# Rounded head outputs in the latents' tiles, a written bank order, and moved transposes and masked copies in layers 2 and 3 of a four-layer model on one core

## The chip, the cores and the metric

The kernel runs on one core of a Trainium2 chip. The metric is the device time of one execution in microseconds: everything from the inputs in device memory to the output in device memory, measured over several runs. The profile is that of one further execution.

## What is computed

A token sequence of 256 positions and width 1024 goes through four layers in fp32. Layers 0 and 1 are one kind of block (adaptive modulation, windowed attention with sinks, a pooling mixer, a gated feed-forward). Layers 2 and 3 are the other kind, and the change is in them alone:

```python
for l in range(DEPTH):
    h = rmsnorm(x, attn_norm[l])
    z = h @ w_in[l]
    (c_q, c_kv, k_rope, g_q, g_k, g_v, g_lr, g_g, r_q, r_k, r_v, r_g) = jnp.split(z, split_points, axis=-1)
    y_a = mla_branch(c_q, c_kv, k_rope, ...)      # 4 heads: queries, keys and values from normalized latents
    y_a = head_rmsnorm(y_a, mla_out_norm[l]).reshape(B, S, MLA_HEADS * MLA_V)
    y_b = gla_branch(g_q, g_k, g_v, g_lr, g_g, ...)   # gated linear attention, 4 heads
    y_c = retention_branch(r_q, r_k, r_v, r_g, ...)   # retention with fixed decay, 4 heads
    x = x + jnp.concatenate([y_a, y_b, y_c], axis=-1) @ w_out[l]
    h = rmsnorm(x, ffn_norm[l])
    u = h @ ffn_w_up[l]
    a, bv = u[..., :D_FF_2], u[..., D_FF_2:]
    a = causal_dwconv(a, ffn_conv_w[l], ffn_conv_b[l])
    x = x + (jax.nn.silu(a) * bv) @ ffn_w_down[l]
```

The first branch is softmax attention over latents (256 positions, two blocks of 128 queries); each of the other two ends in a normalization over its heads and a multiplication with silu of a gate.

## The kernel before, in words

**Products.** Every large fp32 product is made of three matmuls on operands that are split in a high part, rounded to the reduced fp32 form, and a low part, the rest: high by low, low by high, high by high (`exact`, L490 to L492). Weights stream through four raw slots. For each unit of weights ScalarE writes the high half (`prepare`, L1133) and VectorE the low half (`lo`, L1576), two instructions of 1024 columns each; TensorE waits for the second low half (`weights`). A raw slot is loaded again by SyncE once VectorE's low halves are done. Activations are split in the same way, into `in_hi` and `in_lo`, or for the latents into `cn_hi` and `cn_lo`. Small products (scores, rotations, transposes) are plain fp32: `group` (L497), `transposes` (L539), the two rotations (L828, L833).

**The order of the work** is written out by hand, for each engine apart; engines meet by semaphores. In `attention_mixed`, TensorE's order in each of layers 2 and 3 is: latents turned, `gqk`, `rqk`, the rope part of the queries (`qr`) and the rest (`qn`), keys `kn` and values `vm` out of one unit `ukv`, three blocks of attention scores, the gate logits (`ggate`), the values `gv`, the retention scores (four, from the masked keys `kbd`, which lie in `c_row`), the values `rv`, the head outputs of retention (`rout`, L879 and L880), the gate scores (four, from `kbd` again), the attention outputs (from `probT2`), the head outputs of the gate branch (`gout`), the gate product 0 (`gg`), four sums of squares over the heads (L928), the gate product 1 (`rg`), and the output projection `into_y` with the units `wo` 0, 1, 3, 2. Between these stand the transposes of the three blocks of probabilities, `turn_prob(0)` to `turn_prob(2)`.

**Banks.** `take` gives each product the next bank of a rotation that `banks(...)` sets, and waits until the former tenant of the bank has been read. The rotation in this stretch is 4, 5, 1, 0, 3, 2, 6, 7, over and over.

**VectorE** rotates the retention queries and keys, writes the four masked copies `kbd` (L1958), then the low halves of `ukv`; it scales scores and finds their extremes (`softmax`, L1732, L1735), divides by the sums (`normalize`, L1739, L1741; its result is what `turn_prob` waits for), makes the gate queries and keys (L1993, L1999), and at the end scales the head outputs (`head_norm`, L2016) and writes their low parts (`cat_lo`, L1722). **ScalarE** makes the exponentials, copies banks to memory (L1211), takes the root of the sums of squares (L1456, L1459) and rounds the scaled head outputs into `in_hi` (`round_cat`, L1216). The head outputs are eight tiles: 0 to 3 of the attention, 4 and 5 of the gate branch, 6 and 7 of retention. `in_hi` and `in_lo` hold the layer's normalized input until the last gate product has read it, so ScalarE waits for that product before it rounds the first tile:

```python
                sc.wait_ge(*due("gate", L, 1))
                round_cat(L, (0, 1, 2, 3))
```

`cn_hi` and `cn_lo` are five tiles each, whose place in memory the probabilities `prob2` and their transposes `probT2` use after the latents; the last reader of those are the attention outputs.

## Time and profile before

| | |
|---|---|
| median of 3 runs | 1191.18 us (1190.67 to 1191.89) |
| the profiled execution | 1190.44 us, span 1188.6 us from first to last instruction |
| TensorE busy | 1145.2 us, 96% of the span |
| VectorE busy | 809.1 us, 68% |
| ScalarE busy | 634.3 us, 53% |
| GpSimd busy | 25.6 us, 2% |
| mean granted clock of TensorE | 0.998 |
| layer 2, attention part | about 590 to 690 us |
| layer 3, attention part | about 895 to 995 us |

The profiler's names: PE is TensorE, DVE VectorE, ACT ScalarE, SP SyncE, POOL GpSimd. Times count from the span's start. A row of the view in order of time gives start, duration, engine, line, operation, output and inputs, shapes, a count of merged instructions and, in brackets, the idle time before it and what ended that. Matmuls overlap: a row's duration is longer than the distance to the next start, and their ends are modelled. An fp32 matmul shows as two.

### The profile page before, as it was taken

The page shows a single profiled execution, that of the slowest core. Times are in us where ns is not written, and L with a number is a line of the kernel's source. Part 1 is how long each engine was busy: PE and PEld are TensorE (multiplying, and loading weights), DVE is VectorE, ACT ScalarE, POOL GpSimd, SP SyncE. Part 2 cuts the span into 40 slices and gives each one's busy share as a digit, 9 for nine tenths or more (in the row PEclk, how much of TensorE's full clock was granted, in tenths as well). Part 3 has the DMA queues.
Part 4 walks back from the last instruction along what each step waited for, and adds up shares of the span by engine and source line. Part 5 has one row for each costly group of instructions (what it writes and reads, how often), then busy time and mean ns, then how long its engine had stood idle before and what let it go on. Part 6 is the DMA issues. An engine that isn't in the chain of part 4 may idle for free.

```text
span 1188.6 us, 19635 instructions
## 1 busy us (share of the span) xinstructions
PE 1145.2 (96%) x7899; PEld 1024.6 (86%) x7899; DVE 809.1 (68%) x1255; ACT 634.3 (53%) x1114; POOL 25.6 (2%) x61
## 2 busy tenths in 40 slices
PE   5989999999999999999999999999999999999997
PEld 3556999998878999999888799999989889999996
DVE  5798966797986755655676667666566757765663
ACT  3067443456557644435655766555556577555543
POOL 2200000000000000000000000000000000000000
PEclk9999999999999999999999999999999999999999
DMA  9994999997543766585343355544544434555530
GB/s 376 410 420 193 333 324 298 320 377 277 190 154 117 282 236 227 206 265 174 126 178 107 142 206 183 207 178 178 180 141 156 144 106 178 212 179 190 198 106 36
DMA packets 37305, 252.97 MB, mean 213 GB/s; under 512 B 4416, under 2 KB 4704, under 8 KB 8928
## 3 DMA queue, kind: packets, MB, share of 16 engines
q1 hardware_dynamic: 34992, 244.47, 57.2%
q0 software_dynamic: 2080, 7.25, 1.6%
q8 instruction: 63, 1.03, 0.4%
q14 instruction: 26, 0.21, 0.1%
q10 hardware_dynamic: 144, 0.00, 0.0%
HBM read 250.64 MB, written 1.06 MB: 212 GB/s over the span
## 4 chain that ended last, share of the span: by engine, by line
PE 84%; DVE 8%; DMA 3%; ACT 3%; issue 1%; SPq 0%; DVEq 0%; ACTq 0%
PE bank L490 25%; PE bank L492 25%; PE bank L491 25%; PE bank L497 3%; DMA raw_w<-weights 3%; DVE raw_w L1586 2%; PE bank L585 2%; PE bank L539 2%; DVE lo_w L1576 2%; PE bank L628 1%; ACT gtok L1138 1%; PE bank L928 1%; DVE prob L1732 1%; DVE tok L1795 0%; DVE smax L1735 0%
## 5 line engine op out<-in xcount | busy, mean ns | idle before, releaser
L1576 DVE TENSOR_TENSOR lo_w<-raw_w,hi_w 128x1024 fp32r<-128x1024 f32 (+3 forms) x346 | 408.9, 1209 | 124.3 <-ACT hi_w L1133 123.8
L1133 ACT ACTIVATE hi_w<-raw_w 128x1024 fp32r<-128x1024 f32 (+3 forms) x346 | 350.5, 1041 | 151.3 <-DMA raw_w<-weights 88.2
L490 PE MATMUL bank<-in_hi,lo_w 128*128 128x256 f32 x1408 | 395.8, 281 | 0.0
L491 PE MATMUL bank<-in_lo,hi_w 128*128 128x256 f32 x1408 | 392.9, 279 | 0.0
L492 PE MATMUL bank<-in_hi,hi_w 128*128 128x256 f32 x1408 | 392.9, 279 | 0.0
L490 PEld LDWEIGHTS bank<-in_hi,lo_w 128*128 128x128 f32 x1408 | 264.3, 188 | 2.5 <-issue 0.8
L491 PEld LDWEIGHTS bank<-in_lo,hi_w 128*128 128x128 f32 x1408 | 263.6, 187 | 1.9 <-issue 0.5
L492 PEld LDWEIGHTS bank<-in_hi,hi_w 128*128 128x128 f32 x1408 | 264.7, 188 | 0.0
L490 PE MATMUL bank<-hi_w,in_lo 128*128 128x256 f32 (+2 forms) x464 | 143.9, 310 | 8.6 <-DVE in_lo L1687 2.4
L492 PE MATMUL bank<-hi_w,in_hi 128*128 128x256 f32 (+2 forms) x464 | 141.0, 304 | 0.0
L491 PE MATMUL bank<-lo_w,in_hi 128*128 128x256 f32 (+2 forms) x464 | 140.8, 303 | 0.0
L490 PE MATMUL bank<-hi_w,hid_lo 128*128 128x512 f32 x352 | 139.5, 396 | 0.5 <-DVE hid_lo L2059 0.5
L491 PE MATMUL bank<-lo_w,hid_hi 128*128 128x512 f32 x352 | 139.0, 395 | 0.0
L492 PE MATMUL bank<-hi_w,hid_hi 128*128 128x512 f32 x352 | 139.0, 395 | 0.0
L1586 DVE SCALAR_TENSOR_TENSOR raw_w<-raw_w,c_row 128x1024 f32<-128x1024 f32 x96 | 113.5, 1221 | 25.1 <-DMA raw_w<-weights 24.7
L490 PEld LDWEIGHTS bank<-hi_w,in_lo 128*128 128x128 f32 x464 | 87.8, 189 | 17.8 <-issue 9.0
L492 PEld LDWEIGHTS bank<-hi_w,in_hi 128*128 128x128 f32 x464 | 87.9, 189 | 4.6
L491 PEld LDWEIGHTS bank<-lo_w,in_hi 128*128 128x128 f32 x464 | 87.9, 189 | 4.2
L492 PEld LDWEIGHTS bank<-hi_w,hid_hi 128*128 128x128 f32 x352 | 66.1, 188 | 16.0
L490 PEld LDWEIGHTS bank<-hi_w,hid_lo 128*128 128x128 f32 x352 | 66.1, 188 | 15.2 <-DVE hid_lo L2059 0.6
L491 PEld LDWEIGHTS bank<-lo_w,hid_hi 128*128 128x128 f32 x352 | 66.1, 188 | 14.2
L1494 ACT ACTIVATE shared<-bank,vcol 128x256 f32<-128x256 f32 x44 | 24.8, 564 | 98.6 <-PE bank L492 90.8
(216 smaller groups left out, 1080.0 us busy)
## 6 DMA issues: line engine op xcount, KB each, us to landing
raw_w<-weights SPq DMA_DIRECT2D x215, 1024.0 KB, 5.7
ink<-ink_w SPq DMA_DIRECT2D x8, 640.0 KB, 13.2
rows<-norm_rows POOLq DMA_DIRECT2D x5, 512.0 KB, 4.9
ink<-whole_w SPq DMA_DIRECT2D x2, 1024.0 KB, 23.1
early_out<-whole_w SPq DMA_DIRECT2D x2, 1024.0 KB, 13.9
rows<-mod_rows POOLq DMA_DIRECT2D x4, 512.0 KB, 9.2
raw_w<-weights SPq DMA_DIRECT2D x2, 832.0 KB, 4.4
const<-const_table SPq DMA_DIRECT2D x1, 1538.0 KB, 8.0
```

Source lines behind the costliest of these rows:

```text
L490: nc.tensor.matmul(o, st[1], mv[0], start=start, stop=False, **kw)
L491: nc.tensor.matmul(o, st[0], mv[1], start=False, stop=False, **kw)
L492: return nc.tensor.matmul(o, st[0], mv[0], start=False, stop=stop, **kw)
L497: last = nc.tensor.matmul(o, w, r, start=(i == 0), stop=(i == len(pairs) - 1))
L539: last = nc.tensor.transpose(b[:, P * i:P * (i + 1)], s_, k("ident"))
L585: done = nc.tensor.matmul(ps(job)[:, :], half(raw[:, 2 * u + n, :], T), whole[u][:, n, cols(c)], start=(u == 2 and n == 0), stop=(u == 1 a ...
L628: last = nc.tensor.matmul(b[:, P * i:P * (i + 1)], modcol[:, ROWS[(L, kind, w)], t:t + 1].to_broadcast([P, P]), k("ident"), start=True, st ...
L928: nc.tensor.matmul(b[:, :], k(ones), head_sq[:, m, :], start=True, stop=True).then_inc(*sig("hsum", L, n))
L1133: nc.scalar.activation(hi_w[:, m % NSPLIT, cut], raw_view(unit)[:, cut], ACT.Identity).then_inc(*sig("hi_w", unit, i))
L1494: nc.scalar.activation(conv[:, f % 2, :], ps(("gu", L, f))[:, 0:256], ACT.Identity, bias=v(f"conv_b{l}", f), scale=v(f"conv_w{l}", 44 + f) ...
L1576: nc.vector.tensor_tensor(lo_w[:, m % NSPLIT, cut], raw_view(unit)[:, cut], hi_w[:, m % NSPLIT, cut].bitcast(F32), ALU.subtract).then_inc( ...
L1586: ins = nc.vector.scalar_tensor_tensor(w, w, 1.0, c_row[:, :], ALU.mult, ALU.mult, accum_out=mods[:, l, 2 * n + f:2 * n + f + 1])
```

## The change

Five things, all in `attention_mixed` of layers 2 and 3.

1. The rounded head outputs of tiles 0 to 3 and their low parts go to `cn_hi` and `cn_lo`; the units `wo` 0 and 1 of the output projection read them there. ScalarE's wait for the last gate product in front of the rounding is gone. Tiles 4 to 7 go to `in_hi` and `in_lo` as before.
2. The rotation of banks is a list of 31 numbers, one for each product from `rqk` to `gout`.
3. TensorE's order: `turn_prob(1)` stands right behind the `rv` product, ahead of the wait for the copy of its result; `turn_prob(2)` stands ahead of the gate scores.
4. With it, ScalarE copies the second transposes ahead of the high halves of `wo` 0, and VectorE normalizes block 2 ahead of the gate queries and keys.
5. VectorE writes the low halves of `ukv` ahead of the masked keys of retention.

```diff
-            def mixed_wait(L):
-                return (lambda t: pe.wait_ge(*due("cat_lo", L, t))), (lambda t: t), both
+            def mixed_wait(L, unit):
+
+                return (lambda t: pe.wait_ge(*due("cat_lo", L, t))), (lambda t: t), ((cn_hi, cn_lo) if L >= 2 and unit[2] < 2 else both)
...
-                banks(4, 5, 1, 0, 3, 2, 6, 7)
+                banks(4, 5, 1, 0, 3, 2, 6, 7, 4, 5, 1, 0, 3, 2, 6, 7, 4, 5, 1, 0, 2, 3, 6, 0, 7, 4, 5, 1, 2, 3, 0)
                 product(("rqk", L), ("rqk", L, 0), both)
...
                 turn_prob(0)
                 token_values("rv")
+                turn_prob(1)
                 pe.wait_ge(*due("rv_in", L))
                 head_outputs(("rout", L), "ratt", 256)
-                turn_prob(1)
+                turn_prob(2)
...
                     last.then_inc(*sig(*job))
-                turn_prob(2)
...
-            def round_cat(L, tiles):
+            def round_cat(L, tiles, dst):
                 for t in tiles:
                     sc.wait_ge(*due("cat_raw", L, t))
-                    nc.scalar.activation(in_hi[:, t, :], raw[:, t, :], ACT.Identity).then_inc(*sig("cat_hi", L, t))
+                    nc.scalar.activation(dst[:, t, :], raw[:, t, :], ACT.Identity).then_inc(*sig("cat_hi", L, t))
...
                 values("rv", 256)
+                probT_in(1)
                 prepare(("wo", L, 0))
                 head_in(("rout", L), 3)
-                probT_in(1)
                 probT_in(2)
...
-                sc.wait_ge(*due("gate", L, 1))
-                round_cat(L, (0, 1, 2, 3))
+                round_cat(L, (0, 1, 2, 3), cn_hi)
...
+                lo(("ukv", L, 0))
                 for hd in range(4):
                     last = nc.vector.tensor_scalar(kbd[:, hd, :], rk, k("headmask", hd, hd + 1), 32.0 ** -0.5, ALU.mult, ALU.mult)
                 last.then_inc(*sig("rkbd", L))
-                lo(("ukv", L, 0))
...
                 lo(("rg", L, 0))
+                normalize(L, 2, *args(2), prob2, 2)
 
                 ve.wait_ge(*due("gexp", L))
...
                 last.then_inc(*sig("gkbd", L))
-                normalize(L, 2, *args(2), prob2, 2)
...
-                cat_lo(L, (0, 1, 2, 3))
+                cat_lo(L, (0, 1, 2, 3), cn_hi, cn_lo)
```

(`cat_lo` takes its tiles as arguments in the same way as `round_cat`.) Lines of the changed file from `mixed_wait` to `round_cat` stand one lower than before.

How the change moves instructions, in layer 2; layer 3 has the same. In brackets stands what an instruction waits for by name. `bank0` to `bank7` are the banks, `prob2` the probabilities, `vgr` the copied values, `poolw` the gate queries, `c_row` the masked keys.

TensorE, the transposes of block 0 and the first `rv` product, before and then changed:

```order
L497 MATMUL bank1<-gr,c_row 128x256 [waits scored]
L497 MATMUL bank1<-gr,c_row 128x128
L539 MATMUL bank0<-const,prob2 128x128 [waits scored,prob]
L539 MATMUL bank0<-const,prob2 128x128 x3
L490 MATMUL bank3<-hi_w,in_lo 128x256 [waits lo_w,scored]
L491 MATMUL bank3<-lo_w,in_hi 128x256
```

```order
L497 MATMUL bank1<-gr,c_row 128x256 [waits scored]
L497 MATMUL bank1<-gr,c_row 128x128
L539 MATMUL bank0<-const,prob2 128x128 [waits scored,prob]
L539 MATMUL bank0<-const,prob2 128x128 x3
L490 MATMUL bank2<-hi_w,in_lo 128x256 [waits lo_w,ggate_in]
L491 MATMUL bank2<-lo_w,in_hi 128x256
```

The bank of `rv` was the one of attention score 2, to be scaled (`scored`); it is the one of the gate logits (`ggate_in`).

TensorE behind the last `rv` product: retention's head outputs, transposes of block 1, the first gate scores. Before:

```order
L879 MATMUL bank2<-gr,vgr 64x256 [waits ratt,ggate_in,rv_in]
L880 MATMUL bank2<-gr,vgr 64x128
L879 MATMUL bank2<-gr,vgr 64x256 [waits ratt]
L880 MATMUL bank2<-gr,vgr 64x128
L879 MATMUL bank2<-gr,vgr 64x256 [waits ratt]
L880 MATMUL bank2<-gr,vgr 64x128
L879 MATMUL bank2<-gr,vgr 64x256 [waits ratt]
L880 MATMUL bank2<-gr,vgr 64x128
L539 MATMUL bank6<-const,prob2 128x128 [waits gv_in,prob]
L539 MATMUL bank6<-const,prob2 128x128 x3
L497 MATMUL bank7<-poolw,c_row 64x256 [waits ratt,gkbd]
L497 MATMUL bank7<-poolw,c_row 64x256
```

Changed:

```order
L539 MATMUL bank3<-const,prob2 128x128 [waits scored,prob]
L539 MATMUL bank3<-const,prob2 128x128 x3
L880 MATMUL bank6<-gr,vgr 64x256 [waits ratt,gv_in,rv_in]
L881 MATMUL bank6<-gr,vgr 64x128
L880 MATMUL bank6<-gr,vgr 64x256 [waits ratt]
L881 MATMUL bank6<-gr,vgr 64x128
L880 MATMUL bank6<-gr,vgr 64x256 [waits ratt]
L881 MATMUL bank6<-gr,vgr 64x128
L880 MATMUL bank6<-gr,vgr 64x256 [waits ratt]
L881 MATMUL bank6<-gr,vgr 64x128
L539 MATMUL bank0<-const,prob2 128x128 [waits probT_in,prob]
L539 MATMUL bank0<-const,prob2 128x128 x3
```

The transposes of block 1 stand ahead of the head outputs and those of block 2 ahead of the gate scores, which begin two rows later.

VectorE, behind the rotation of the retention queries and keys, and then behind the low halves of `rg`:

```order
 L1750 TENSOR_TENSOR gr<-gr,const 128x512
 L1751 TENSOR_TENSOR gr<-gr,tmp 128x512
-L1958 TENSOR_SCALAR c_row<-gr,const 128x256 x4
-L1576 TENSOR_TENSOR lo_w<-raw_w,hi_w 128x1024 x2
+L1576 TENSOR_TENSOR lo_w<-raw_w,hi_w 128x1024 x2
```

```order
-L1993 TENSOR_TENSOR poolw<-poolw,gr 128x128
-L1993 TENSOR_TENSOR poolw<-poolw,gr 128x64
-L1995 MEMSET poolw 128x64
-L1999 SCALAR_TENSOR_TENSOR c_row<-gr,const,hidden 128x256 x4
 L1739 RECIPROCAL ssum<-ssum 128x4
 L1741 TENSOR_TENSOR prob<-prob,ssum 128x512
+L1994 TENSOR_TENSOR poolw<-poolw,gr 128x256
+L1994 TENSOR_TENSOR poolw<-poolw,gr 128x192
+L1996 MEMSET poolw 128x64
+L1994 TENSOR_TENSOR poolw<-poolw,gr 128x128
+L1994 TENSOR_TENSOR poolw<-poolw,gr 128x64
+L1996 MEMSET poolw 128x64
```

The two low halves of `ukv` pass the masked copies, and the reciprocal and the product of `normalize` pass ten instructions of the gate queries and keys.

## Rows read from the trace of the kernel before

**Rows 1.** TensorE's waits, 592 us to the end: in all, times, longest (us).

```profile
PE bank L490 <- DVE in_lo L1722: 2.1, 2, 1.1
PE bank L490 <- DVE prob L1732: 1.8, 2, 0.9
PE bank L490 <- DVE lo_w L1576: 1.6, 2, 0.8
PE bank L497 <- ACT probT L1211: 1.6, 2, 0.8
PE bank L879 <- ACT vgr L1211: 1.4, 2, 0.7
```

**Rows 2.** TensorE in order of time (start, duration), around L828 and L833.

```profile
605.07 1.02 PE L828 MATMUL bank<-gr,const 128*128 128x512 f32 x2
...
606.04 0.28 PE L491 MATMUL bank<-cn_lo,hi_w 128*128 128x256 f32 x1
...
610.16 1.02 PE L833 MATMUL bank<-mla,const 128*128 128x512 f32 x2
...
612.17 0.28 PE L491 MATMUL bank<-cn_lo,hi_w 128*128 128x256 f32 x1
```

**Rows 3.** VectorE in order of time, ahead of the keys' products.

```profile
608.31 1.14 DVE L1958 TENSOR_SCALAR c_row<-gr,const 128x256 f32<-128x256 f32 x4
609.36 2.36 DVE L1576 TENSOR_TENSOR lo_w<-raw_w,hi_w 128x1024 fp32r<-128x1024 f32 x2
```

**Rows 4.** TensorE in order of time: transposes, then products.

```profile
576.93 0.66 PE L539 MATMUL bank<-const,normed 128*128 128x128 f32 x4
...
577.54 0.28 PE L491 MATMUL bank<-lo_w,in_hi 128*128 128x256 f32 x1
...
631.68 0.60 PE L539 MATMUL bank<-const,prob 128*128 128x128 f32 x4
...
633.38 0.28 PE L491 MATMUL bank<-lo_w,in_hi 128*128 128x256 f32 x1
```

**Rows 5.** TensorE in order of time, from the retention values' last product.

```profile
638.59 0.28 PE L492 MATMUL bank<-hi_w,in_hi 128*128 128x256 f32 x1
639.55 0.66 PE L879 MATMUL bank<-gr,vgr 128*64 128x256 f32 x4 [0.69 <-ACT vgr L1211]
...
641.05 0.66 PE L539 MATMUL bank<-const,prob 128*128 128x128 f32 x4
641.64 2.82 PE L497 MATMUL bank<-poolw,c_row 128*64 128x256 f32 x32
644.39 0.66 PE L539 MATMUL bank<-const,prob 128*128 128x128 f32 x4
645.83 0.35 PE L497 MATMUL bank<-probT,mla 128*128 128x128 f32 x1 [0.78 <-ACT probT L1211]
```

**Rows 6.** VectorE in order of time, around the gate keys.

```profile
637.80 0.69 DVE L1993 TENSOR_TENSOR poolw<-poolw,gr 128x256 f32<-128x256 f32 x2 [0.91 <-ACT hidden L1434]
...
638.83 1.60 DVE L1999 SCALAR_TENSOR_TENSOR c_row<-gr,const,hidden 128x256 f32<-128x256 f32 x4
...
640.55 0.69 DVE L1741 TENSOR_TENSOR prob<-prob,ssum 128x512 f32<-128x512 f32 x1
```

**Rows 7.** TensorE in order of time, last gate product to output projection.

```profile
664.90 0.28 PE L492 MATMUL bank<-in_hi,hi_w 128*128 128x256 f32 x1
666.24 0.47 PE L490 MATMUL bank<-hi_w,in_lo 128*128 128x512 f32 x1 [1.06 <-DVE in_lo L1722]
```

**Rows 8.** ScalarE and VectorE in order of time, rounding of heads 0 to 3.

```profile
665.22 1.34 ACT L1216 ACTIVATE in_hi<-raw 128x256 fp32r<-128x256 f32 x4 [3.15 <-PE bank L492]
...
665.67 1.44 DVE L1722 TENSOR_TENSOR in_lo<-raw,in_hi 128x256 fp32r<-128x256 f32 x4 [2.68 <-ACT in_hi L1216]
```

**Rows 9.** TensorE at the start of the program, and one stretch's busy times and granted clock.

```profile
12.48 3.47 PE L539 MATMUL bank<-const,normed 128*128 128x128 f32 x16 [0.34 <-DVE normed L1662]
...
639.55:650.17 10.62, 9.84 (x96) 7.91 (x96) 6.38 (x15) 4.61 (x7) 0.00 (x0) 1.00 0.29 101
```

More of the change, by code:

```diff
@@ L546, in turn_norm, with down_wait @@
                     transposes(("tr", N, T, c), [normed[:, 512 * c + P * i:512 * c + P * (i + 1)] for i in range(4)])
-            def mixed_wait(L):
-                return (lambda t: pe.wait_ge(*due("cat_lo", L, t))), (lambda t: t), both
-            def down_wait(L):
+            def mixed_wait(L, unit):
+                return (lambda t: pe.wait_ge(*due("cat_lo", L, t))), (lambda t: t), ((cn_hi, cn_lo) if L >= 2 and unit[2] < 2 else both)
+            def down_wait(L, unit):
                 return (lambda t: pe.wait_ge(*due("hid_lo", L, t))), (lambda t: t % RING), (hid_hi, hid_lo)
             def into_y(L, w, unit, T, first=False, last=False, before_last=None):
-                wait, slot, src = (mixed_wait, down_wait)[w](L)
+                wait, slot, src = (mixed_wait, down_wait)[w](L, unit)
                 wt = weights(unit, ("y", L, w, T, 1) if last else ("used", unit))
@@ L1469, in attention_mixed @@
                 sc.preload_act_table_set("natural_log_exp_and_others")
-                round_cat(L, (6, 7, 4, 5))
+                round_cat(L, (6, 7, 4, 5), in_hi)
                 prepare(("wo", L, 2))
@@ L1717, in boundary, with cat_lo @@
                 behind(units[1])
-            def cat_lo(L, tiles):
+            def cat_lo(L, tiles, hi, lo_):
                 for t in tiles:
                     ve.wait_ge(*due("cat_hi", L, t))
-                    nc.vector.tensor_tensor(in_lo[:, t, :], raw[:, t, :], in_hi[:, t, :].bitcast(F32), ALU.subtract).then_inc(
+                    nc.vector.tensor_tensor(lo_[:, t, :], raw[:, t, :], hi[:, t, :].bitcast(F32), ALU.subtract).then_inc(
                         *sig("cat_lo", L, t))
@@ L2029, in attention_mixed @@
                         nc.vector.tensor_tensor(raw[:, t, :], raw[:, t, :], gates[:, t - 4, :], ALU.mult).then_inc(*sig("cat_raw", L, t))
-                cat_lo(L, (6, 7, 4, 5))
+                cat_lo(L, (6, 7, 4, 5), in_hi, in_lo)
                 lo(("wo", L, 2))
```

## The prediction

> **What bounds the kernel now.** I read the page's busy shares first: TensorE is at work for 96% of the span, no other engine for more than 68%, so the time is TensorE's own products plus what it waits for. Then the waits of TensorE from 592 us to the end, which hold layers 2 and 3 whole: there are only five kinds, each met twice (once a layer), 8.5 us in all [rows 1]. Between and behind them, through both feed-forwards, there is no other. So in this half of the program every microsecond that TensorE does not lose there comes off the span, and nothing else does. Last I read TensorE's order of time around each of the five, in layer 2; layer 3 repeats it, 305 us later, with the same figures, which is why each sum below is taken twice. The ends of matmuls are modelled and a wait hides part of the fill of the products behind it, so I measure each loss from start to start, against a place where the same succession runs without a wait.
>
> **The change, part by part.**
>
> (a) The weights' low halves for the keys and values are now computed ahead of the masked retention keys. Behind the rotation product L828, which nothing holds up, the second product of the next group starts 0.97 us after the rotation's start (605.07 to 606.04). Behind L833 it starts 2.01 us after (610.16 to 612.17) [rows 2]. Lost: 1.04 us. The wait is for VectorE, whose two low halves run from 609.36 for 2.36 us, behind four masked copies that began at 608.31 [rows 3]. The second product followed their end (611.72) by 0.45 us. Swapped, the halves end 1.05 us sooner, at 610.67, so the second product could start at 611.12, and without any wait it would at 611.13. I take all of 1.04, and 0.8 as the least, should the two not meet so closely. The masked copies then end about where the halves ended, so the rotation of the queries behind them starts where it did, and the retention scores that read the copies come five groups of products later. Cost of the swap: nothing; without that cover it would be the copies' 1.1 us.
>
> (b) The banks. The value product of retention was given bank 3, where the attention score of block 2 lay until VectorE had scaled it. Four transposes and the second product behind them are 1.70 us apart (631.68 to 633.38); the same pair without a wait 0.61 (576.93 to 577.54) [rows 4]. Lost: 1.09 us. It now takes bank 2, whose gate logits VectorE takes out while the gv product runs. The other new places (3 for the second transposes, 6 for the retention outputs, 0 for the third transposes, then 2, 3 and 0) are emptied by copies and scalings that stand, in ScalarE's and VectorE's order, well before TensorE comes to them; the nearest is bank 3, scaled at the time at which the value product was held until now, with that whole product in between. All of 1.09 counts.
>
> (c) The second transposes stand ahead of the wait for the values' copy. The last value product starts at 638.59, so the next slot is 638.71; the head outputs start at 639.55, released by ScalarE's copy [rows 5]. Lost: 0.84 us. The four transposes cost 0.59 us wherever they stand (641.05 to 641.64) [rows 5]. In the hole they are free: 0.59 saved, 0.25 us of waiting left.
>
> (d) The third transposes move ahead of the 32 gate score passes, so their copy is long in place when the attention outputs want it. Those began 1.44 us after the transposes (644.39 to 645.83) instead of 0.59 [rows 5]. Saved: 0.85 us. On ScalarE the second copy moves ahead of two weight halves and the third is still behind them; the gate scores' 2.75 us (641.64 to 644.39) lie between the transposes and their reader now, and cover it.
>
> What (d) costs: VectorE must normalize block 2 before the gate queries and keys instead of behind them: 0.81 us, from the gate keys' end at 640.43 (638.83 plus 1.60) to 641.24 (640.55 plus 0.69) [rows 6]. It has a hole there: 0.91 us idle ahead of 637.80, waiting for ScalarE's exponentials. So the gate keys come 1.04 us sooner, at 639.39. TensorE comes to them at 639.51: 638.71 less 2.13 (a and b), transposes to 637.17, head outputs at 637.42, 1.50 us for those, 0.59 for the third transposes. A margin of 0.12 us is thin, since a product does not start at the very end of what it waits for; a wait of 0.1 to 0.2 us may appear, and I leave it out of the sum.
>
> (e) Head outputs 0 to 3 are rounded into the latents' tiles, which nobody reads any more, so ScalarE need not wait for the last gate product. That product's last matmul starts at 664.90 and the output projection at 666.24, a loss of 1.22 us past the next slot at 665.02 [rows 7]. ScalarE sat idle for 3.15 us before rounding and VectorE, idle for 2.68 us before 665.67, had its normalized heads at 662.99 [rows 8]. Unheld, the first rounded tile and its rest (about 0.4 us more, a quarter of the four tiles' 1.44) stand at about 663.4, 1.6 us before TensorE wants them; moved along with TensorE's other savings, the margin stays, since this chain starts from TensorE's own sums of squares. All of 1.22 counts. Behind it ScalarE's and VectorE's work for tiles 4 to 7 moves ahead by more than TensorE does. No transfer is issued from another place; SyncE's wait for a free weight slot ends with VectorE's low halves, which only come sooner.
>
> The sum is 1.04 + 1.09 + 0.59 + 0.85 + 1.22 = 4.79 us a layer, 9.58 us in all. The profiled execution took 1190.44 us, so 1180.9; the median of the runs is 0.74 above it: **1181.6 us**. By what the list of waits calls idle, the sum would be 8.5 less some 0.5 that stays at (c): 8.0 us, 1183.2 at the median. I take the starts, since (a) and (b) show the second product late by more than the idle time says. The Trainium skill (Perfetto Trace Analysis, Tensor Engine Instruction) says that a matmul's end in a profile is estimated and not observed; that speaks for the sum by starts, and the trace agrees, with 1.04 us at (a) against 0.8 listed as idle.
>
> **The rivals.**
>
> R1, the chain of the heads takes the gate product's place: (e) stays, because the normalized heads, not the bank or the buffer, come last. For it: four square roots, products and rounding run in single file on two engines. Against it: the 3.15 us that ScalarE idled. It would leave 7.14 us of gain: 1184.0.
>
> R2, VectorE comes late to the gate keys: the normalization finds no hole, or its wait for the exponentials holds up what is queued behind it. It decides as soon as the keys end later than 639.5 by layer 2's clock; at worst TensorE loses the 0.81 us in each layer, 1.6 in all: 1183.2. For it: the margin of 0.12 us.
>
> R3, the gain is given back: TensorE, earlier by 4.8 us, meets weights that are not ready in the feed-forward, and the end stands where it was: 1191. For it: ScalarE waits for transfers elsewhere. Against it: in the two feed-forwards TensorE waited for nobody at all [rows 1].
>
> R4, slower: the clock of TensorE drops to its lower level in the stretch of small products and transposes, 639.55 to 650.17, where the order changes. The first transposes of the program, after 11 us without work, took 3.47 us for 16, so 0.22 us each, and the ones at 631.68 took 0.60 for four, 0.15 [rows 4, 9]: the slow level shows there, though the view grants 1.00. At 1.2 GHz instead of 2.4 this stretch costs up to its own 10.6 us again; it turns the sign once it costs over 4.8. Two layers: 1190.4 + 2 x (10.6 - 4.8) + 0.7 = 1202.7. Against it: the stretch was granted 1.00 with all its waits in it [rows 9], and the change takes waits out. The Trainium skill (TensorE: Matmul & The Clock Gate, Part 4: PE-mode transpose) says that transposes don't count as work for the clock in the way that products do; by that rule this stretch is the one at risk, and the trace of before doesn't bear it out, with 1.00 granted.
>
> **How the numbers follow.** I give the forecast 0.74, R1 0.08, R2 0.08, R3 0.06 and R4 0.04. The forecast's own range: with the 0.25 us at (c) gone too, 10.1 us and 1181.1; with the lower end of (a) and 0.2 us of waiting in (d), 8.7 us and 1182.5. The runs before spread by 0.7 below and above, so it starts at 1180.5. R1 and R2 reach to 1184.0, and both together to 1185.6; I end the range at 1185.5, which leaves out R3 and R4, 1 in 10. A difference under 0.2%, 2.4 us, could hardly be told from none. The forecast, R1 and R2 are all faster by more than that: 0.90. R3 is the same: 0.06. R4 is slower: 0.04.
>
> **What would show it.** A span near 1179.0. TensorE's list of waits from 592 us on without the low halves, the scaled score, the transposed probabilities and the rounded heads, and with 0.1 to 0.3 us a layer for the values' copy and perhaps as much for the gate keys. In layer 2 the rotation L834 to the second product behind it should take 0.97, the last gate product should end near 661.6 with the output projection right behind it, and ScalarE should round four tiles before that. I am wrong if a bank's former tenant appears as a releaser, if the gate keys hold TensorE for over 0.3 us, or if the feed-forward shows a wait that it did not have.

## The result, and the profile after

| | before | changed |
|---|---|---|
| median of the runs | 1190.93 us (1190.37 to 1191.89, 4 runs) | 1178.9 us (1178.76 to 1183.38, 4 runs) |
| ratio | | 0.991, 95% interval 0.9892 to 0.9929 |
| profiled execution: time, span | 1190.44, 1188.6 us | 1183.38, 1181.3 us |
| TensorE busy in the span | 96% | 97% |

The change is faster by 12.0 us at these medians, where 9.6 were forecast, and 1178.9 lies below the forecast's range (1180.5 to 1185.5). Note that the profiled execution of the changed kernel is the slowest of its four runs; that will matter.

First the waits of TensorE from 592 us to the end (in all, times, longest), where before there were five kinds and 8.5 us [rows 1]:

```profile
PE bank L880 <- ACT vgr L1212: 0.5, 2, 0.3
```

One is left, the one that the forecast left: 0.25 us a layer for the copy of the retention values. Neither the gate keys nor a bank's former tenant nor a feed-forward has come in. TensorE of the changed kernel in order of time (start, duration), at the places of [rows 2, 4, 5, 7]:

```profile
612.35 1.02 PE L834 MATMUL bank<-mla,const 128*128 128x512 f32 x2
...
613.33 0.28 PE L491 MATMUL bank<-cn_lo,hi_w 128*128 128x256 f32 x1
...
632.98 0.60 PE L539 MATMUL bank<-const,prob 128*128 128x128 f32 x4
...
633.54 0.28 PE L491 MATMUL bank<-lo_w,in_hi 128*128 128x256 f32 x1
...
638.88 0.60 PE L539 MATMUL bank<-const,prob 128*128 128x128 f32 x4
639.73 0.66 PE L880 MATMUL bank<-gr,vgr 128*64 128x256 f32 x4 [0.25 <-ACT vgr L1212]
...
641.23 0.66 PE L539 MATMUL bank<-const,prob 128*128 128x128 f32 x4
641.82 2.82 PE L497 MATMUL bank<-poolw,c_row 128*64 128x256 f32 x32
644.57 2.16 PE L497 MATMUL bank<-probT,mla 128*128 128x128 f32 x17
...
663.67 0.28 PE L492 MATMUL bank<-in_hi,hi_w 128*128 128x256 f32 x1
663.79 0.39 PE L490 MATMUL bank<-hi_w,cn_lo 128*128 128x512 f32 x1
664.02 0.40 PE L491 MATMUL bank<-lo_w,cn_hi 128*128 128x512 f32 x1
```

From the rotation to the second product behind it 0.98 us (before 2.01), from the transposes to the second product 0.56 (1.70), the attention outputs right behind the gate scores, the output projection 0.12 us behind the last gate product (1.34). Of the heads, ScalarE and VectorE show the second half of [rows 8]:

```profile
660.73 1.32 ACT L1217 ACTIVATE cn_hi<-raw 128x256 fp32r<-128x256 f32 x4
...
661.66 1.43 DVE L1722 TENSOR_TENSOR cn_lo<-raw,cn_hi 128x256 fp32r<-128x256 f32 x4
```

Both now run on without waiting; a quarter of VectorE's 1.43 us past 661.66 the first tile is whole, at 662.02, 1.8 us before TensorE takes it up.

So every wait went as forecast, and the time did not come out as forecast. What a layer's edits are worth is to be had apart from the rest of the program, by the distance between two matmuls that are the same in all kernels: TensorE's matmuls stand in a fixed order and number (7,899), and I cut the program at numbers 1600, 3700, 4500, 5700 and 6700. Microseconds between their starts:

| | layer 0 | layer 1 | attention 2 | feed-forward 2 | attention 3 | feed-forward 3 |
|---|---|---|---|---|---|---|
| before, first profile | 267.2 | 306.0 | 115.87 | 166.6 | 144.45 | 170.8 |
| before, second profile | 267.3 | 304.1 | 115.87 | 166.0 | 144.30 | 171.4 |
| changed, first profile | 271.2 | 304.5 | 110.95 | 166.6 | 139.33 | 171.4 |
| changed, second | 268.4 | 304.2 | 110.96 | 165.9 | 139.58 | 170.8 |
| changed, third | 267.6 | 304.4 | 110.96 | 165.9 | 139.36 | 170.8 |

Between them the two attention parts are shorter by 9.6 to 10.0 us, and the forecast's sum was 9.58. Layers 0 and 1, whose code the change does not touch, differ together by up to 3.7 us between executions of one kernel. One cause is seen in the windows (busy time of PE, PEld, DVE, ACT, POOL; then the granted clock). Before, first profile:

```profile
342.00:346.00 4.00, 2.16 (x10) 1.57 (x9) 1.97 (x5) 4.00 (x14) 0.00 (x0) 1.00 0.00 0
346.00:350.00 4.00, 4.00 (x13) 3.08 (x12) 3.96 (x7) 2.22 (x3) 0.00 (x0) 0.58 0.29 84
```

The same kernel, its second profile:

```profile
342.00:346.00 4.00, 2.18 (x10) 1.56 (x10) 1.99 (x5) 4.00 (x14) 0.00 (x0) 1.00 0.00 0
346.00:350.00 4.00, 4.00 (x19) 3.23 (x18) 3.95 (x7) 2.01 (x3) 0.00 (x0) 1.00 0.41 106
```

TensorE did the same in the 4 us ahead, busy for 2.16 and 2.18 us; once the clock fell to its lower level (1.2 instead of 2.4 GHz) and 13 matmuls started in the next window, once it did not and 19 did. The layer took 305.99 against 304.14 us: 1.85 us for this stretch. The profiled execution of the changed kernel had two of them in layer 0, at 52.6 and 66.2 us, and none here:

```profile
50.00:54.00 4.00, 2.43 (x10) 1.68 (x11) 3.69 (x16) 1.19 (x2) 0.00 (x0) 0.82 1.01 418
54.00:58.00 4.00, 4.00 (x9) 1.39 (x8) 3.28 (x8) 0.45 (x2) 0.00 (x0) 0.75 1.01 422
64.00:68.00 4.00, 1.66 (x6) 1.58 (x7) 3.96 (x8) 4.00 (x13) 0.00 (x0) 0.78 1.03 426
68.00:72.00 4.00, 4.00 (x15) 2.80 (x15) 3.90 (x10) 2.55 (x9) 0.00 (x0) 0.79 1.02 424
```

The Trainium skill (TensorE: Matmul & The Clock Gate, Part 1) says of the start of a kernel that the number of matmuls at the lower level varies from run to run. The rows above show such a variation in the middle of one: a stretch of 3.4 us at the lower level in one execution and none in the other.

### The profile page after: what moved, and what is told of

Same layout as the page of the kernel before. It is cut to its first block, busy times and chain, and to the rows that moved or that the text cites. A ratio compares the mean times of both kernels' runs of the same rounds, so it can differ in the third digit from the quotient of the medians.

```text
span 1181.3 us, 19635 instructions
## 1 busy us (share of the span) xinstructions
PE 1145.1 (97%) x7899; PEld 1025.8 (87%) x7899; DVE 808.8 (68%) x1255; ACT 632.7 (54%) x1114; POOL 28.3 (2%) x61
## 3 DMA queue, kind: packets, MB, share of 16 engines
q8 instruction: 63, 1.03, 0.3%
## 4 chain that ended last, share of the span: by engine, by line
PE 78%; DVE 10%; DMA 7%; ACT 4%; issue 2%; SPq 0%; DVEq 0%; ACTq 0%
PE bank L490 22%; PE bank L492 22%; PE bank L491 22%; DMA raw_w<-weights 7%; DVE lo_w L1576 3%; DVE raw_w L1586 3%; PE bank L497 3%; PE bank L586 2%; PE bank L539 2%; ACT gtok L1139 1%; PE bank L629 1%; ACT hi_w L1134 1%; PE bank L929 1%; ACT prob L1252 0%; PE bank L689 0%
## 5 line engine op out<-in xcount | busy, mean ns | idle before, releaser
L490 PE MATMUL bank<-hi_w,in_lo 128*128 128x256 f32 (+2 forms) x432 | 130.1, 301 | 4.7 <-DVE in_lo L1687 2.4
L1586 DVE SCALAR_TENSOR_TENSOR raw_w<-raw_w,c_row 128x1024 f32<-128x1024 f32 x96 | 113.3, 1219 | 25.2 <-DMA raw_w<-weights 25.0
L492 PE MATMUL bank<-hi_w,in_hi 128*128 128x256 f32 (+2 forms) x432 | 127.4, 295 | 0.0
L491 PE MATMUL bank<-lo_w,in_hi 128*128 128x256 f32 (+2 forms) x432 | 127.4, 295 | 0.0
L490 PEld LDWEIGHTS bank<-hi_w,in_lo 128*128 128x128 f32 x432 | 81.5, 189 | 11.6 <-issue 6.5
L492 PEld LDWEIGHTS bank<-hi_w,in_hi 128*128 128x128 f32 x432 | 81.5, 189 | 2.9
L491 PEld LDWEIGHTS bank<-lo_w,in_hi 128*128 128x128 f32 x432 | 81.3, 188 | 2.6
```

The source lines that it names most:

```text
L490: nc.tensor.matmul(o, st[1], mv[0], start=start, stop=False, **kw)
L491: nc.tensor.matmul(o, st[0], mv[1], start=False, stop=False, **kw)
L492: return nc.tensor.matmul(o, st[0], mv[0], start=False, stop=stop, **kw)
L1586: ins = nc.vector.scalar_tensor_tensor(w, w, 1.0, c_row[:, :], ALU.mult, ALU.mult, accum_out=mods[:, l, 2 * n + f:2 * n + f + 1])
```

## The experiments

The question was whether each part is worth its term, alone and in company, and where the other 2 to 3 us come from. Twelve further runs were made, r1 to r12, on four occasions and three chips, each beside runs of the kernel before on the same chip; r1, r2 and r9 are the two kernels as they are.

**Is the slow stretch part of the kernel before?** r1_before has no edit.

> The kernel before, unchanged, to see how its own runs spread and where TensorE's clock falls. Theory F (free): the 3.4 us stretches at the lower clock that the two profiles show in layers 0 and 1 (one at 346.6 us before; two at 52.6 and 66.2 us after the change) fall at random, cost 1.5 us each, and have nothing to do with the change. Then some runs of this kernel should come without one and stand near 1189, with a mean clock of 0.999, and its median may lie anywhere from 1189 to 1191. Theory T (tied): the drop in layer 1 belongs to this kernel and the changed one is free of it. Then all of its runs stand at 1190.4 to 1191.9 and its profile shows the drop near 346 us again.

Measured: 1189.27 us (12 runs, 1188.27 to 1193.58), beside 25 more runs of the same kernel at 1189.98 (1188.27 to 1192.5); ratio 0.9996 (0.9987 to 1.0005). Its profile, shown above, has no slow stretch in layer 1. So the stretch falls in some executions and not in others, which refutes theory T. Of the 14 profiles of all kernels two have it (the first of the kernel before and that of r4); layer 1 takes 305.9 and 306.0 us in these and 303.9 to 304.6 in the other twelve. The forecast's 1190.44 was one that had it.

**The change again**, on that chip:

> The changed kernel, unchanged. By my sum layers 2 and 3 give 9.6 us; the trace of the changed kernel shows 4.96 and 4.51. By theory F its runs spread between 1178.8 (no drop) and 1183.4 (two in layer 0), and where its profile has no drop, layers 0 and 1 take the time of the kernel before less 1.7 us. By theory T layer 1 is faster by 1.7 us in each run. In both the difference of the medians is 9.5 plus the difference in drops: 11 to 12 us.

Measured: 1179.39 us (4 runs), ratio 0.9905 (0.9892 to 0.9918), 10.6 us at the medians, under the 11 to 12 expected. Its parts are the table's row "changed, second". Its profile has two slow stretches in layer 0, at 18.4 and 66.2 us, and yet took 1179.35 us and not the 1183.4 that theory F gave to two.

**Part (e) alone:**

```diff
-                return (lambda t: pe.wait_ge(*due("cat_lo", L, t))), (lambda t: t), both
+                return (lambda t: pe.wait_ge(*due("cat_lo", L, t))), (lambda t: t), ((cn_hi, cn_lo) if L >= 2 and unit[2] < 2 else both)
...
-                sc.wait_ge(*due("gate", L, 1))
-                round_cat(L, (0, 1, 2, 3))
+                round_cat(L, (0, 1, 2, 3), cn_hi)
```

> The kernel before with the rounding of head outputs 0 to 3 into the latents' tiles alone. My sum gives 1.22 us a layer, 2.4 us in all: 1188.5. If the head chain takes the gate product's place (R1), nothing.

Measured: 1187.39 us, ratio 0.9978 (0.9969 to 0.9987). The wait for the low parts of the rounded heads is gone from the list, so R1 did not occur.

**The turns alone**, (c) and (d):

```diff
                 token_values("rv")
+                turn_prob(1)
                 pe.wait_ge(*due("rv_in", L))
                 head_outputs(("rout", L), "ratt", 256)
-                turn_prob(1)
+                turn_prob(2)
```

> The kernel before with the turns alone: transposes 1 and 2 earlier, their copy, and the normalization of block 2 earlier; banks in the old rotation, so the rv product still waits for bank 3. My sum gives 0.59 + 0.85 = 1.44 us a layer, 2.9 in all: 1188.0. If VectorE comes late to the gate keys (R2), 0.8 us a layer less: 1189.6.

Measured: 1186.93 us, ratio 0.9971 (0.9961 to 0.9981). No wait for the gate keys is listed. (Not shown in this diff: the moves of (d) on ScalarE and VectorE, as in the whole change.)

**Part (a) alone:**

```diff
+                lo(("ukv", L, 0))
                 for hd in range(4):
...
                 last.then_inc(*sig("rkbd", L))
-                lo(("ukv", L, 0))
```

> Only part (a): the low halves for the keys and values ahead of the masked retention keys, everything else as before. Two readings of what this wait costs. By starts (the forecast's way): rotation L834 to the second product behind it falls from 2.01 to 0.97 us, 1.04 us a layer, so each attention part of layers 2 and 3 (before: 115.9 and 144.4 us) shortens by about 1.0 and the whole by 2.1, ratio 0.9983. By the list of waits: 0.8 us a layer, 1.6 in all. Rival: part of it comes back at the next wait (the bank of the retention values, 1.09 us a layer), since that is set by VectorE's scaling of block 2 and not by TensorE: then the later wait grows by what this one lost, and the attention part shortens by clearly less than 1.04. VectorE's own order of time is nearly unmoved by the swap, so if its scaling of block 2 stands where it stood, the rival is right and the parts are worth less alone than together.

Measured: 1188.45 us, ratio 0.9981 (0.9969 to 0.9994). The wait for the bank stands as before (1.7, 2, 0.9), so nothing came back there.

**Part (b) alone:**

```diff
-                banks(4, 5, 1, 0, 3, 2, 6, 7)
+                banks(4, 5, 1, 0, 3, 2, 6, 7, 4, 5, 1, 0, 3, 2, 6, 7, 4, 5, 1, 0, 2, 3, 6, 7, 4, 5, 1, 0, 2, 3, 6)
```

> Only part (b): the bank order written out, with the retention values in bank 2. If the loss of 1.09 us a layer is the bank's alone, the wait for the scaled score goes and the attention parts shorten by 1.09 each, 2.2 in all, ratio 0.9982. Rival: with the values' product earlier by 1.1 us, ScalarE's copy of it and the gate keys of VectorE (which end at 640.4 us by the clock of before) are not earlier, so the waits behind it, 0.84 us for the copy and none for the gate keys, grow: then under 1.09 a layer, down to 0.5.

Measured: 1187.21 us, ratio 0.9972 (0.996 to 0.9984). Its waits of TensorE from 592 us on, where the one for the bank (1.8, 2, 0.9 in [rows 1]) is missing and the others stand as before:

```profile
PE bank L490 <- DVE in_lo L1722: 2.1, 2, 1.1
PE bank L490 <- DVE lo_w L1576: 1.7, 2, 0.9
PE bank L497 <- ACT probT L1211: 1.6, 2, 0.8
PE bank L879 <- ACT vgr L1211: 1.4, 2, 0.7
```

**Each of two parts taken out of the whole.** r7 is the changed kernel with the old rounding, r8 the changed kernel with the old `banks(4, 5, 1, 0, 3, 2, 6, 7)`.

> The whole change without (e): the head outputs are rounded into the old tiles again, behind the last gate product. If the parts add up, the attention parts shorten by 9.8 - 2.7 = 7.1 us in both layers together (3.6 and 3.5), ratio 0.9940 to the kernel before, and TensorE's list of waits from 592 us on holds the low halves of the rounded heads (0.5 to 0.7 us a layer) beside the values' copy. Rival, by the size that stands in the list of waits for (e): only about 1 us a layer is missing, 7.8 of gain. Rival 2: (e) is worth more in the whole change than alone, because the earlier attention outputs leave the gate product more exposed: less than 6.5 us of gain.

> The whole change without (b): the old rotation of banks under the new order of turns, so the retention values come to a bank that still holds an attention score or a piece of another job. If the bank's wait is worth its 1.09 us a layer, the gain falls from 9.8 to 7.6 us, ratio 0.9936. Rival: in the new order the old rotation meets other former tenants, and since the turns moved ahead, TensorE waits for the scaled score by more than 1.09 (up to 1.04 more, what (a) saved just ahead of it): gain 5.5 to 6.5 us. The list of waits names the line that empties the bank.

Measured: r7 1182.3 us, ratio 0.9929 (0.9902 to 0.9955); r8 1182.36 us, ratio 0.9924 (0.9899 to 0.995). Waits of r7, then of r8:

```profile
PE bank L490 <- DVE in_lo L1722: 2.1, 2, 1.1
PE bank L879 <- ACT vgr L1211: 0.5, 2, 0.2
```

```profile
PE bank L490 <- DVE prob L1731: 1.7, 2, 0.9
PE bank L879 <- ACT vgr L1211: 0.5, 2, 0.3
```

The intervals of both hold what was expected (0.9940 and 0.9936), and the rivals' times in part. The medians can't tell terms of 2 us from one another; the starts can. I took four stretches that hold one part each, in every kernel and both layers: from the rotation L833 to three matmuls further, from the first transposes of the probabilities to the second product behind them, from inside the values' product to the attention outputs, and from the last gate products to the sixteenth product of the output projection. Shorter than in r1_before by (us; both layers agree within 0.01), and in the last column the whole attention parts of layers 2 and 3, between the cuts of the first table:

| | (a) | (b) | (c) and (d) | (e) | attention 2, 3 |
|---|---|---|---|---|---|
| forecast, a layer | 1.04 | 1.09 | 1.44 | 1.22 | |
| (a) alone | 1.03 | 0 | 0 | 0 | 0.73, 0.95 |
| (b) alone | 0 | 1.14 | 0 | 0 | 1.13, 0.67 |
| turns alone | 0 | 0 | 1.40 | 0 | 1.27, 1.40 |
| (e) alone | 0 | 0 | 0 | 1.35 | 1.36, 1.27 |
| all but (e) | 1.03 | 1.14 | 1.40 | 0 | 3.42, 3.23 |
| all but (b) | 1.03 | 0 | 1.40 | 1.35 | 3.64, 3.56 |
| changed, three profiles | 1.03 | 1.14 | 1.40 | 1.35 | 4.91 to 4.92, 4.72 to 4.97 |

(In the (a) column one entry of (b) alone, in layer 3, reads 0.09 longer.) In these stretches the parts add up and do not touch one another: no loss comes back at the next wait, as r5's and r6's rivals had it, and none is worth more in company. 1.03 + 1.14 + 1.40 + 1.35 = 4.92 us a layer, 9.84 in both.

The whole attention parts are not that exact. The four parts alone add up to 8.8 us there, where the changed kernel has 9.6 to 9.9, and "all but (e)" has 6.65 where 7.1 was expected. The lists of waits don't account for that. Most of it is pace: products follow one another more closely in some kernels and layers than in others, without a wait, as the last section shows. The (e) column holds a piece of it. Against r1_before the projection's first product starts 1.22 us sooner, its second 1.30, the sixteenth 1.35, and from the 49th to the last all start 1.49 sooner.

**What is outside the attention parts.** The changed kernel once more, and both kernels with the wait ahead of layer 1's slow stretch filled with seven products that nobody reads:

```diff
+                    if first and (L, w, T, c) == (1, 0, 0, 0):
+                        for _ in range(7):
+                            nc.tensor.matmul(ps(job)[:, :], wt[0][:, 0, 0:P], wt[0][:, 0, 0:512], start=True, stop=True)
```

> The changed kernel once more, beside the two filled ones, on their chip and in their rounds. If the base level is what failed in the forecast, the difference to the kernel before is that of the attention parts, 9.7 to 10.0 us, with the rest scattered by where the clock drops: ratio 0.9915 to 0.9920. If there is a further gain that the parts don't show, the ratio comes out at 0.9900 again, as in the first comparison.

> The changed kernel with seven products more in layer 1, written into a bank that is started anew behind them, in the 1.8 us in which TensorE waits for the low halves ahead of the output projection (at 343 us). They take 7 x 0.234 = 1.6 us of a wait. If the clock's drop at 346 us comes from that stretch's idleness, no run has it any more and the median falls by up to 1 us against the unfilled kernel. If the drop is as rare here as the two profiles of the changed kernel say (none of two), or has another cause, nothing changes: within 0.5 us. If the fill is late, it costs up to 1.6 us.

> The kernel before with the same seven products. Its profiled execution held 3.4 us at half the clock at 346 us, right behind this wait, and about half of its timed runs have a mean clock of 0.996 or less and stand 1.5 to 2 us above the rest. If the idle stretch ahead is the cause, those runs go: median 1188.5 to 1189.0 instead of 1190.0 to 1190.4, ratio 0.9985, and the profile shows 1.00 granted from 338 to 350 us. If it has another cause, the share of such runs stays: ratio 1.000.

Measured: r9 1178.85 us (5 runs), ratio 0.991 (0.9896 to 0.9923); r10 1179.73 (5 runs), 0.9911 (0.9899 to 0.9924); r11 1189.22 (11 runs, 1187.67 to 1191.3), 0.9992 (0.9983 to 1.0001), beside 1190.01 for the kernel before. The fill did what it should in the window (r10, the row that answers to 342 to 346 above):

```profile
342.00:346.00 4.00, 3.88 (x17) 2.98 (x18) 1.93 (x6) 4.00 (x15) 0.00 (x0) 1.00 0.00 0
346.00:350.00 4.00, 4.00 (x19) 3.21 (x18) 3.96 (x8) 2.65 (x3) 0.00 (x0) 1.00 0.24 59
```

r9's ratio lies between the two that were expected, 0.9915 and 0.9900, and its interval holds both. The fill did not settle the cause. The clock stayed up, but it stayed up here in 10 of the 12 profiles without the fill too; r11's 0.8 us are within its interval of nothing, and r10 is no faster than r9. Nor did the premise hold that about half of the runs of the kernel before have a mean clock of 0.996 or less: on this chip it was 1 of 15. r11's own profile had two slow stretches in layer 0 and took 270.5 us there. Filling one hole of several is no version worth having.

**The margin at the gate keys.** The third transposes as well go ahead of the wait for the copy:

```diff
                 turn_prob(1)
+                turn_prob(2)
                 pe.wait_ge(*due("rv_in", L))
                 head_outputs(("rout", L), "ratt", 256)
-                turn_prob(2)
```

> The changed kernel with the third transposes too ahead of the wait for the values' copy (banks 0 and 6 exchanged to suit). It tries the margin at the gate keys. In the changed kernel VectorE ends those at 638.94 us and TensorE comes to the gate scores at 639.05, a margin of 0.11 us. Here the 0.25 us of waiting for the values' copy would go, so TensorE would come to the gate scores at 638.80, 0.14 before the keys' end. If R2's mechanism is real, a wait for the gate keys of 0.15 to 0.4 us a layer takes the place of the copy's, and the attention parts stay at 111.0 and 139.4 us within 0.2. If the margin is larger than read, both waits are gone and each part shortens by 0.25. The time: within 0.5 us of the changed kernel's 1179, ratio 0.991, in either case, so the list of waits and the parts decide, not the median.

Measured: 1180.62 us (4 runs), ratio 0.9914 (0.9897 to 0.993); attention parts 111.04 and 139.29. TensorE's waits from 592 us, and its order of time in layer 2:

```profile
PE bank L497 <- DVE c_row L2000: 0.7, 2, 0.3
```

```profile
637.99 1.03 PE L539 MATMUL bank<-const,prob 128*128 128x128 f32 x8
638.96 0.66 PE L880 MATMUL bank<-gr,vgr 128*64 128x256 f32 x4
...
640.87 2.82 PE L497 MATMUL bank<-poolw,c_row 128*64 128x256 f32 x32 [0.34 <-DVE c_row L2000]
```

VectorE beside it:

```profile
639.21 1.60 DVE L2000 SCALAR_TENSOR_TENSOR c_row<-gr,const,hidden 128x256 f32<-128x256 f32 x4
```

The copy's wait is gone and the gate keys' has come: they end at 640.81, the scores start 0.06 us later. From the values' product to the attention outputs this is 1.46 us a layer shorter than before, where the changed kernel has 1.40. So R2's mechanism is real, and 0.25 us of waiting moved buys 0.06.

## Why the prediction was wrong, point by point

**The level failed first, and the sum by little.** The step that failed is "The profiled execution took 1190.44 us, so 1180.9; the median of the runs is 0.74 above it", with "The runs before spread by 0.7 below and above, so it starts at 1180.5". It takes the sum off a level that three runs gave, and so hands on to the changed kernel all the slow stretches that these runs had. The profiled execution itself held 1.85 us of them, in the windows of the page that I was not reading since they lie outside the changed layers. Over the 71 runs of the kernel before on three later occasions (r1's own 12 and the 25, 19 and 15 beside the others) the median is 1190.01 us, the fastest 1188.27, the slowest 1195.46. From the three I had read a band of 1.2 us; it is 7. From 1190.01 the forecast's own sum gives 1180.4, at the lower end of its range. (With the 11 runs beside the first comparison and beside r12 the median is 1190.24, and the sum gives 1180.7.)

The level can be taken out by two profiles in which the clock fell nowhere but in the last few microseconds, r1's of the kernel before at 1188.27 us and r9's of the changed one at 1178.41. They are 9.86 us apart: 9.85 in the attention parts, and the sum of layers 0 and 1 and both feed-forwards is equal within 0.2 us. Three of the four runs of the result (1178.76 to 1179.01) stand close to that 1178.41, while the four of the kernel before stand 2 to 4 us above 1188.27.

So of the 2.7 us by which 1181.6 missed 1178.9, 1.2 are the level (1191.18 for 1190.01) and 0.3 the sum. The last 1.3 are open, as said below: the four runs of the kernel before in the result had no better level (median 1190.93), and from them the right sum would have given 1181.1.

**The sum was short by 0.3 us** in 9.6: (a) 1.04 for 1.03 and (c) and (d) 1.44 for 1.40 were right, (b) 1.09 should have been 1.14, and (e) 1.22 should have been 1.35. At (b) I took the undisturbed succession from another place ("against a place where the same succession runs without a wait"): transposes to second product take 0.56 us here, not the 0.61 of [rows 4]. At (e) 1.22 was right for the first product's start and ended there. The first product behind the wait of before is 0.31 us ahead of the second (666.24 to 666.55), and in the changed kernel 0.23 (663.79 to 664.02), which is the other 0.08, as "a wait hides part of the fill of the products behind it" had warned:

```profile
666.24 0.47 PE L490 MATMUL bank<-hi_w,in_lo 128*128 128x512 f32 x1 [1.06 <-DVE in_lo L1722]
666.55 0.40 PE L491 MATMUL bank<-lo_w,in_hi 128*128 128x512 f32 x1
```

The rest, 0.05 by the sixteenth product and 0.19 by the 49th, is a closer succession of the products, for which the sum had no term. The other reading, by the list of waits (8.0 us), is refuted: 9.6 to 10.0 came. This was where the Trainium skill (Perfetto Trace Analysis, Tensor Engine Instruction) was weighed, with its rule that a matmul's end in a profile is an estimate; the runs agree, with 1.03 us at (a) against 0.8 listed.

**What remains.** 1190.01 less 9.84 is 1180.17; the 13 runs of the changed kernel have a median of 1179.01 (1178.29 to 1183.38). The difference of the two sets of runs is 10.7 us by their means, with a 95% interval of 9.8 to 11.5 (both sets drawn again at random 5,000 times), and 9.98 by their fastest; the 11 further runs of the kernel before move it to 10.8. So the parts' 9.84 lies within what the runs allow, at its edge. That slow stretches fall less often in the changed kernel is not shown. By the record of mean clocks it is 0.996 or less in 3 of 13 runs, against 24 of 71, but of the 71 that share went from 1 in 15 to 10 in 19 with the chip and the occasion. The profiles point the other way in layer 0: five of the changed order (three profiles, r10 and r12) hold seven slow stretches there, three of the kernel before (two profiles and r11) hold two. Whether the last 1 us or so is chance or not stays open.

**The rivals.** R1 (the heads' chain comes last) fell: the first tile has a margin of 1.8 us, against 1.6 forecast, and (e) alone gave its whole term. R2 (VectorE late at the gate keys) did not occur, by a margin that was forecast at 0.12 us. In the changed kernel's third profile the rows are:

```profile
636.66 1.60 DVE L2000 SCALAR_TENSOR_TENSOR c_row<-gr,const,hidden 128x256 f32<-128x256 f32 x4
```

```profile
638.36 1.95 PE L497 MATMUL bank<-poolw,c_row 128*64 128x256 f32 x20
```

The keys end at 638.26, TensorE comes 0.10 us later, with no wait listed; r12 showed a start 0.06 us after such an end. My 0.1 to 0.2 us of possible waiting was not needed, by 0.04 us. R3 (given back in the feed-forward) fell: no wait there, and those parts differ by 0.6 us between executions of either kernel. R4 (slower, the clock) fell. The stretch of turns, in the changed kernel's first profile:

```profile
638.88:649.34 10.46, 10.21 (x101) 8.24 (x100) 7.48 (x21) 5.60 (x10) 0.00 (x0) 1.00 0.36 111
```

Granted 1.00. The Trainium skill (TensorE: Matmul & The Clock Gate, Part 4: PE-mode transpose), by which transposes do not count as work for the clock as products do, made no difference here: with eight transposes within these 10.5 us it stayed at 1.00. The start of the program speaks against that rule. The first 19 matmuls (L539) are all transposes, the next one starts some 2 us behind the last of them, and in r2's profile the starts of these transposes lie 213 ns apart up to 14.89 us and 109 ns apart from 15.04 us on. The clock rose with nothing but transposes run.

## What to carry to other kernels

Where a matmul engine runs in a fixed order, measure an edit between two of its instructions that both kernels share: over stretches of a few microseconds, terms of 1.0 to 1.4 us came out to 0.01 in every kernel here, while whole-program medians of the same runs could not tell them apart. Keep the two instructions close: over a whole attention part the same terms were off by up to 0.5 us (0.67 for 1.14). Read a loss from start to start, at its own place if another kernel shows that place without the wait. And before a forecast is tied to a measured time, look through the whole span, the parts outside the change above all, for what this one execution happened to suffer, and don't take three runs' spread for the kernel's.

## What the runs showed of the hardware that I had not expected

The clock fell or did not behind the same work: after 2.16 us busy of 4 it fell at 346 us, after 2.18 of 4 it did not, and the fall there cost 1.85 us. In layer 0 it fell near 18, 53 or 65 us, in one or two of these places in eleven of the 14 profiles. What it cost depends on the place, though each lasted 3.4 us. Layer 0 took 267.2 to 267.6 us without one, 267.1 with one at 18.4 us (r4), 267.4 to 268.5 with one near 65 (in five of these six profiles the clock is recorded as up only from 20.6 to 21.0 us on), 268.4 with two, at 18.4 and 66.2 (r2), and 270.4 to 271.2 with two near 53 and 66.

And TensorE has two paces with the clock at 1.00 throughout. The products of 128x256, three kinds in turn, in r1_before behind the wait that (a) removes:

```profile
610.78 0.28 PE L490 MATMUL bank<-cn_hi,lo_w 128*128 128x256 f32 x1
...
612.82 0.39 PE L490 MATMUL bank<-hi_w,cn_lo 128*128 128x512 f32 x1
```

and with (a) alone, the last 18 of the same group:

```profile
611.42 0.28 PE L490 MATMUL bank<-cn_hi,lo_w 128*128 128x256 f32 x1
...
613.54 0.40 PE L490 MATMUL bank<-hi_w,cn_lo 128*128 128x512 f32 x1
```

18 products take 2.04 us in the first and 2.12 in the second: 113.3 and 117.8 ns from start to start. The quicker pace came in short stretches, many of them behind a wait or behind small matmuls, and sometimes for longer in a feed-forward (the 0.6 us between 165.9 and 166.6, and 170.8 and 171.4, in the table). The kernels with (a) took 0.19 us more from the attention scores to the first transposes than those without, in 15 of 16 layers: a little of what a wait costs comes back as pace, and (a) alone shortened its attention parts by 0.73 and 0.95 us, not 1.03.

At (e) it goes the other way. In all 14 layers with (e), 48 products of 128x512 in the output projection, those that read the latents' tiles, start 229.3 ns apart, and the next ones, which read `in_hi` and `in_lo`, 233.3. In all 14 layers without (e), where a wait stands ahead of them, all start 233.3 apart. The 48 make 0.19 us a layer, the step from 1.30 to 1.49 above. The tile alone does not set the pace: products of the values out of the same latents' tiles start 233 ns apart in some layers and 229 in others. What switches it was not tried. The Trainium skill (TensorE: Matmul & The Clock Gate, Wait — 56ns, not 53.3ns?) gives for back-to-back matmuls at the upper clock a spacing of the columns over 2.4 GHz and some 2.5 ns; an estimate from that is 109 ns for 256 columns, and both paces measured here are longer.
